# Second attention of a two-block layer: weight pieces over 42 groups, two feature tiles among them, dilated turns in groups 42 to 53

## Chip, cores and metric

The kernel runs on one core of a Trainium2 chip (trn2). The metric is the device time of one execution in microseconds (us); lower is better. Engines: PE (TensorE), DVE (VectorE), ACT (ScalarE), POOL (GpSimd), SP (SyncE, which here only issues the transfers).

## What is computed

One token sequence (512 x 1024, float32) goes through a recurrent layer, a sliding-window attention with sinks, and then a second block, which matters here:

```python
h = rms_norm(x, norm_mix)
proj = h @ w_in
a_q, a_kv, a_g, b_qkv, c_qkv = jnp.split(proj, PROJ_SPLITS, axis=-1)
o_a = nsa_mixer(a_q, a_kv, a_g, ...)       # 4 heads: compressed, selected and window keys
o_b = dilated_mixer(b_qkv, ...)            # 3 dilations x 2 heads, one softmax over all
o_c = stick_breaking_mixer(c_qkv)          # 6 heads, sum of log-failures after each key
x = x + jnp.concatenate([o_a, o_b, o_c], axis=-1) @ w_out
h = rms_norm(x, norm_mlp)
x = x + jnp.square(jax.nn.relu(h @ w_up)) @ w_down
```

## The kernel before, in words

All weights come as units of 128 x 1024 float32. SP loads each into a ring of 4 buffers (`raw`), in the order of the U_ constants (lines 40 to 66); an engine splits it into a rounded high part `wh` and the remainder `wl`; PE multiplies with three matmuls for each product (lines 1236 to 1238: high-high, high-low, low-high). From unit U_GB on POOL makes the splits (`split`, lines 1180 to 1190: a mark, the high part, two halves of the low part). A unit's place is free once PE has counted it in `units_done`, so units are used in the order in which they stand.

The second block's projection consists of token-major groups G0, G4, G1, G2, G3 (4 units each, four token tiles) and feature-major tiles F0 to F6 (1 unit each). F1 and F4, F2 and F5, F3 and F6 are queries and keys of the three stick-breaking head pairs. G1 holds the dilated queries and the gates' logits, G2 the dilated keys, G3 the dilated values. G0, G4, F0, F1, F4, F2, F5 and F3 are multiplied ahead of the second attention. For each F tile DVE scales the bank (`scale_f`, line 2220), ACT writes the high half (`stick_high`, line 1769), DVE the low one (`low_f`, line 2227). The compressed keys are turned once by PE (line 1496) and copied by ACT (line 1807), before the attention's loop.

The second attention (`make_attention(2)`, from line 571) runs over 68 *groups*, each one head's 128 queries against the keys before them: 8 groups of the first stick pair; then 36 groups of the other branch (compressed, selected, window) with the 16 other stick groups among them; and 8 dilated groups (60 to 67). PE, ACT and DVE run the same software pipeline; in *step* i
- PE (line 813): scores of group i + 4, transposes of group i's probabilities (`turn`), their product with the values for group i - 1, then what else is planted at that step;
- DVE (line 1106): bias, mask and maximum for group i + 3 (`mask1`), finishing a head whose last group was i - 2, for a stick group i + 2 the scan over log-failures (`mask2`: lines 1020, 1021, 1025), the copy of even-numbered chunks of transposed probabilities from the bank;
- ACT (line 899): exponentials of group i + 3 (for stick: Abs, Exp, Ln), Exp of a stick group i + 2, the copy of odd-numbered chunks.

A *chunk* is a bank's worth of transposes (up to four blocks), numbered through (`with_chunks`, line 269); even ones lie in bank 3, odd ones in bank 4, and PE waits for chunk c - 2 to be copied before it writes chunk c. Scores go to banks 0, 1, 2 in turn, and from group WIDE_FROM (line 160) on also to bank 7. Until then bank 7 takes the *pieces*: F6, and the G1, G2 and G3 tiles, one token tile in two halves of 12 matmuls each (`piece`, line 1501), at the steps of PIECE_STEPS (line 155). ACT and DVE take a tile one step after its second half (TAKEN, line 157). After G2, `scales` gives the reciprocal norms of the dilated heads.

The twelve dilated tiles (six of queries, six of keys) go through *turns* (TURNS2, line 152): POOL scales and doubles a head pair's rows (`double`, line 1131), PE transposes them as a chunk of its own (`turn_chunk`, line 806, transposes on line 810), ACT copies that chunk one step later (line 915), POOL writes high and low half (`split_dil`, lines 1154 and 1157). There are two buffers: POOL's order is double 0, double 1, split 0, double 2, split 1, and so on. The split of turn 0 waits for the last piece of G3, because the tiles lie where PE's inputs xh and xl were. The dilated groups' scores (from step 56) wait for all twelve. POOL's order is: splits of all units up to G3, the turns, then the units of the output projection (line 1228).

At the end of the loop TAILS (line 164) starts the first output tiles; the output projection and the MLP (from 790 us on) are PE at work without a break.

## Time and profile before

| | |
|---|---|
| median of 3 runs | 1176.36 us (1174.43 to 1176.77) |
| the profiled execution | 1172.59 us, its span 1170.8 us |
| PE busy | 1111.2 us, 95% of the span |
| DVE, ACT, POOL busy | 643.3, 425.5, 529.9 us |
| mean granted PE clock | 0.98 |
| DMA | 97.18 MB, mean 83 GB/s |
| chain that ended last | PE 77%, DVE 12%, ACT 5%, issue 4% |

A time is that of one execution; the span is from the first to the last instruction on the profile. Busy time of PE contains overlap of matmuls in the pipeline. A clock of 1.00 is the upper of PE's two levels (2.4 GHz), 0.5 the lower (1.2 GHz); a mean in between is a mixture in time. In rows, the text in square brackets is how long the engine was idle before an instruction and which one released it; "x12" is a count.

### The profile page before, as it was taken

The numbers are of one execution on the slowest core, as the hardware profiler recorded it, in microseconds if no ns is written. First come the engines' busy times: TensorE is split into PE (matmuls) and PEld (weight loads), VectorE is DVE, ScalarE is ACT, GpSimd is POOL, SyncE is SP. The second block draws the span as 40 slices with busy tenths as digits, with TensorE's granted clock in tenths as the row PEclk, the third lists the DMA queues.
The fourth block names the chain that finished last, engine by engine and source line by source line (L and its number), as shares of the span: only waits on it lengthen the run. The fifth ranks groups of instructions, "written<-read, shape, count | busy, mean of one in ns | idle before, by whom it ended". The sixth has DMA issues, their size and how long they took to land.

```text
span 1170.8 us, 16126 instructions
## 1 busy us (share of the span) xinstructions
PE 1111.2 (95%) x5801; PEld 951.2 (81%) x5801; DVE 643.3 (55%) x1131; ACT 425.5 (36%) x852; POOL 529.9 (45%) x525
## 2 busy tenths in 40 slices
PE   6999999999989999999988977789999999999998
PEld 5788888898779888898888977678878888888887
DVE  6869777677567646484566576845631321321321
ACT  5373668363346532115554565523020110110110
POOL 0000000000443327989454165408976776777772
PEclk9999999999999999999999887899999999999999
DMA  6322322413211002323221000202423223223221
GB/s 247 127 89 90 109 90 90 144 54 126 90 54 38 20 18 72 125 92 127 72 73 55 18 2 1 72 1 91 127 90 100 98 90 108 90 93 104 90 90 54
DMA packets 27280, 97.18 MB, mean 83 GB/s; under 512 B 3024, under 2 KB 3408, under 8 KB 27088
## 3 DMA queue, kind: packets, MB, share of 16 engines
q1 hardware_dynamic: 27216, 96.32, 24.5%
q8 instruction: 41, 0.67, 0.2%
q14 instruction: 23, 0.19, 0.1%
HBM read 94.21 MB, written 2.10 MB: 82 GB/s over the span
## 4 chain that ended last, share of the span: by engine, by line
PE 77%; DVE 12%; ACT 5%; issue 4%; POOL 1%; DMA 1%; SPq 0%; DVEq 0%; POOLq 0%; ACTq 0%
PE bank L1236 22%; PE bank L1238 21%; PE bank L1237 21%; PE bank L788 4%; PE bank L751 4%; PE bank L768 3%; DVE arena L1967 1%; DVE wl L1918 1%; DVE arena L1021 1%; ACT wh L1597 1%; PE bank L810 1%; DVE arena L1006 1%; DMA x<-x_in 1%; POOL wl L1189 0%; DVE arena L2318 0%
## 5 line engine op out<-in xcount | busy, mean ns | idle before, releaser
L1185 POOL TENSOR_TENSOR hold<-hold 128x2 f32<-128x2 f32 x117 | 29.3, 251 | 524.8 <-PE bank L1238 524.8
L1236 PE MATMUL bank<-xh,wh 128*128 128x512 f32 x568 | 226.4, 399 | 12.2 <-DVE xl L1887 9.7
L1238 PE MATMUL bank<-xh,wl 128*128 128x512 f32 x568 | 221.9, 391 | 0.0
L1237 PE MATMUL bank<-xl,wh 128*128 128x512 f32 x568 | 221.9, 391 | 0.0
L1236 PE MATMUL bank<-yh,wh 128*128 128x512 f32 x520 | 203.4, 391 | 2.0 <-DVE yl L2323 1.5
L1238 PE MATMUL bank<-yh,wl 128*128 128x512 f32 x520 | 202.4, 389 | 0.0
L1237 PE MATMUL bank<-yl,wh 128*128 128x512 f32 x520 | 202.3, 389 | 0.0
L1189 POOL TENSOR_TENSOR wl<-raw,wh 128x512 fp32r<-128x512 f32 x117 | 175.3, 1498 | 0.0
L1188 POOL TENSOR_TENSOR wl<-raw,wh 128x512 fp32r<-128x512 f32 x117 | 157.1, 1343 | 9.8
L1236 PEld LDWEIGHTS bank<-xh,wh 128*128 128x128 f32 x568 | 107.2, 189 | 35.5 <-issue 11.9
L1186 POOL TENSOR_SCALAR wh<-raw 128x1024 fp32r<-128x1024 f32 x117 | 126.8, 1084 | 0.0
L1238 PEld LDWEIGHTS bank<-xh,wl 128*128 128x128 f32 x568 | 107.0, 188 | 22.8
L1237 PEld LDWEIGHTS bank<-xl,wh 128*128 128x128 f32 x568 | 107.2, 189 | 21.3 <-issue 0.7
L1236 PEld LDWEIGHTS bank<-yh,wh 128*128 128x128 f32 x520 | 97.6, 188 | 23.2 <-DVE yl L2323 1.9
L1238 PEld LDWEIGHTS bank<-yh,wl 128*128 128x128 f32 x520 | 97.6, 188 | 20.6
L1237 PEld LDWEIGHTS bank<-yl,wh 128*128 128x128 f32 x520 | 97.7, 188 | 19.8
L1851 ACT ACTIVATE arena<-arena 128x512 f32<-128x512 f32 x32 | 20.2, 633 | 243.7 <-DVE arena L2318 243.7
L788 PE MATMUL bank<-arena 128*128 128x64 f32 (+2 forms) x620 | 90.7, 278 | 16.0 <-DVE arena L1081 5.4
L788 PEld LDWEIGHTS bank<-arena 128*128 128x128 f32 x620 | 85.8, 204 | 18.6 <-issue 7.4
L2330 DVE TENSOR_TENSOR x<-bank,x 128x512 f32<-128x512 f32 x32 | 22.1, 692 | 140.8 <-PE bank L1238 140.8
L1918 DVE TENSOR_TENSOR wl<-raw,wh 128x1024 fp32r<-128x1024 f32 x56 | 68.0, 1222 | 40.3 <-ACT wh L1597 40.0
L1236 PE MATMUL bank<-wh,xh 128*128 128x512 f32 (+2 forms) x224 | 85.3, 381 | 0.2
(260 smaller groups left out, 1831.8 us busy)
## 6 DMA issues: line engine op xcount, KB each, us to landing
raw<-weight_units SPq DMA_DIRECT2D x173, 512.0 KB, 3.4
x<-x_in SPq DMA_DIRECT2D x4, 512.0 KB, 8.1
out_fm<-x SPq DMA_DIRECT2D x8, 256.0 KB, 2.0
arena<-tables SPq DMA_DIRECT2D x1, 1024.0 KB, 10.5
...
```

The source lines that it names most:

```text
L751: mm = pe.matmul(out, q, kk, start=t == 0, stop=t == len(terms) - 1 and kind != "stick")
L768: mm = pe.transpose(B[3 + c % 2][:, j * P:(j + 1) * P], col0[:, col:col + P], ident[:])
L788: mm = pe.matmul(out, pt[:, c % slots, j * P:(j + 1) * P], value_ap(g, s_, kb), start=first, stop=total == 0)
L1185: pool.tensor_tensor(hold[:], hold[:], hold[:], ALU.add).then_inc(held, 1)
L1186: pool.tensor_scalar(wh[:, j, :], raw[:, j, :], 1.0, 1.0, ALU.mult, ALU.mult).then_inc(high_done, 1)
L1188: pool.tensor_tensor(wl[:, j, 0:512], raw[:, j, 0:512], wh[:, j, 0:512], ALU.subtract)
L1189: pool.tensor_tensor(wl[:, j, 512:1024], raw[:, j, 512:1024], wh[:, j, 512:1024], ALU.subtract)\
L1236: pe.matmul(out, lh, rh, start=start, stop=False)
L1237: pe.matmul(out, lh, rl, start=False, stop=False)
L1238: return pe.matmul(out, ll, rh, start=False, stop=stop)
L1918: dve.tensor_tensor(wl[:, u % RING, :], raw[:, u % RING, :], wh[:, u % RING, :], ALU.subtract)\
L2330: dve.tensor_tensor(x[:, m, :], B[4 + m % 4][:], x[:, m, :], ALU.add).then_inc(down_read, 1)
```

## The change

It reorders; no arithmetic is added or taken away.
- Pieces lie in steps 1 to 41 and not 0 to 29: G1 at 1 to 8, F3 (in two halves) at 10 and 11, F6 (also in halves) at 12 and 13, G2 at eight steps from 15 to 25, G3 at eight steps from 28 to 41.
- F3 is no longer multiplied before the loop, nor F6 behind the scores of step -2. Their scale, high and low halves on DVE and ACT move along, and their units stand behind those of G1.
- The compressed keys' turn moves from before the loop to the end of PE's step 0, ACT's copy of it to step 1; it uses bank 7 (bank 2 before), F5 bank 5 (bank 0 before), F3 bank 7 (bank 1 before).
- The twelve turns lie in the steps 42 to 53, one in each, and not in every second step from 28 to 50. With a turn's chunk between each two groups' chunks, the chunks of groups 42 to 53 have the numbers 45, 47, ... 67.
- Bank 7 joins the scores at group 47 (step 43), not at group 36 (step 32).

```diff
--- before.py
+++ after.py
@@ -57,10 +57,10 @@
 U_W1 = (U_F4 - 2, U_F4 - 1, U_F4 + 1, U_F4 + 2)
 U_F2 = U_F4 + 3
 U_F5 = U_F2 + 1
-U_F3 = U_F5 + 1
+U_G1 = U_F5 + 1
+U_F3 = U_G1 + 4
 U_F6 = U_F3 + 1
-U_G1 = U_F6 + 1
-U_G2 = U_G1 + 4
+U_G2 = U_F6 + 1
 U_G3 = U_G2 + 4
 U_OUT2 = U_G3 + 4
 U_MLP = U_OUT2 + 8
@@ -149,16 +149,16 @@
 ITEMS1 = {-3: ("gate", 4, 8), 14: ("gate", 5, 6), 30: ("gate", 6, 6), 46: ("gate", 7, 6)}
 
 
-TURNS2 = {28 + 2 * k: key for k, key in enumerate([("q", m) for m in range(6)] + [("k", m) for m in (0, 1, 2, 4, 5, 3)])}
-
-
-PIECE_STEPS = {"G1": (0, 1, 2, 3, 4, 5, 6, 7), "G2": (9, 12, 13, 14, 15, 16, 17, 18), "G3": (20, 23, 24, 25, 26, 27, 28, 29)}
+TURNS2 = {42 + k: key for k, key in enumerate([("q", m) for m in range(6)] + [("k", m) for m in (0, 1, 2, 4, 5, 3)])}
+
+
+PIECE_STEPS = {"G1": (1, 2, 3, 4, 5, 6, 7, 8), "F3": (10, 11), "F6": (12, 13), "G2": (15, 17, 18, 19, 21, 22, 24, 25),
+               "G3": (28, 32, 33, 35, 36, 38, 39, 41)}
 PIECES = {step: (name, q // 2, q % 2) for name, steps in PIECE_STEPS.items() for q, step in enumerate(steps)}
-TAKEN = {PIECE_STEPS[name][2 * t + 1] + 1: (name, t) for name in PIECE_STEPS for t in range(TB)}
+TAKEN = {steps[2 * t + 1] + 1: (name, t) for name, steps in PIECE_STEPS.items() for t in range(len(steps) // 2)}
 GATES_AT = PIECE_STEPS["G1"][-1] + 1
 SCALES_AT = PIECE_STEPS["G2"][-1] + 1
-WIDE_FROM = 36
-F6_HIGH, F6_LOW = 5, 6
+WIDE_FROM = 47
 TURN_LAG, OUT_LAG = 5, 6
 
 TAILS = {1: {-1: ((0, 0, 6),), 0: ((1, 0, 6), (0, 6, 7), (1, 6, 7)), 1: ((2, 0, 4),), TURN_LAG - 1: ((2, 4, 7), (3, 0, 4))},
@@ -197,10 +197,11 @@
     seg2 = [("bout", m, "X") for m in range(8)] + [("G0", t, "A") for t in range(4)] + [("ssq", 2, "N")]
     seg2 += [("F", 0, "D"), ("rstd", 2, "B"), ("F", 1, "D")] + [("G4", t, "A") for t in range(4)]
     seg2 += [("hid", 0, "A"), ("hid", 1, "A"), ("F", 4, "D")] + [("nT", j, "D") for j in range(6)]
-    seg2 += [("hT", 0, "A"), ("F", 2, "D"), ("kc", 0, "A"), ("F", 5, "D"), ("F", 3, "D"), ("kcT", 0, "A"), ("F", 6, "D")]
-    pieces = [(name, t) for name in PIECE_STEPS for t in range(TB)]
-    seg2 += [(name, t, "A") for name, t in pieces]
-    at2 = {key: 7 for key in [("F", 6)] + pieces}
+    seg2 += [("hT", 0, "A"), ("F", 2, "D"), ("kc", 0, "A"), ("F", 5, "D"), ("kcT", 0, "A")]
+    seg2 += [("G1", t, "A") for t in range(TB)] + [("F", 3, "D"), ("F", 6, "D")]
+    seg2 += [(name, t, "A") for name in ("G2", "G3") for t in range(TB)]
+    at2 = {item[:2]: 7 for item in seg2[-15:]}
+    at2["F", 5] = 5
     bank, free, before = {}, {}, {}
     count = {"A": 0, "D": 0}
     for seg, items in ((seg1, ITEMS1), (seg2, {})):
@@ -813,8 +814,6 @@
                 for i in range(-LOOK - 1, ng + OUT_LAG):
                     if 0 <= i + LOOK + 1 < ng:
                         scores(i + LOOK + 1)
-                    if i == -2 and a == 2:
-                        behind_scores()
                     if 0 <= i < ng:
                         turn(i)
                     if 0 <= i - V_LAG < ng:
@@ -830,6 +829,8 @@
                         if q == 0 and before7[key]:
                             pe.wait_ge(*before7[key])
                         item(key, range(KD * q // parts, KD * (q + 1) // parts))
+                    if a == 2 and i == 0:
+                        behind_scores()
                     if a == 2 and i in PIECES:
                         item(*PIECES[i])
                     for m, k0, k1 in TAILS[a].get(i - ng, ()):
@@ -899,12 +900,14 @@
                 for i in range(-LOOK, ng + OUT_LAG):
                     if 0 <= i + LOOK < ng:
                         soft1(i + LOOK)
-                    if a == 2 and i in TAKEN:
+                    if a == 2 and i == 1:
+                        behind_scores()
+                    if a == 2 and i in TAKEN and TAKEN[i][0][0] == "G":
                         item(TAKEN[i])
-                    if a == 2 and i == F6_HIGH:
-
-                        act.wait_ge(s["scores"], groups[7]["strip0"] + 1)
-                        item(("F", "high"))
+                    if a == 2 and i - 1 in TAKEN and TAKEN[i - 1][0][0] == "F":
+                        if TAKEN[i - 1][0] == "F6":
+                            act.wait_ge(s["scores"], groups[7]["strip0"] + 1)
+                        item(TAKEN[i - 1])
                     if a == 2 and i == SCALES_AT + 1:
                         item(("scales", 0))
                     if a == 2 and i - 1 in TURNS2:
@@ -916,8 +919,6 @@
                                        scale=scale).then_inc(chunk_taken(chunk_of[name, m])[0], 1)
                     if 0 <= i + LOOK - 1 < ng:
                         soft2(i + LOOK - 1)
-                    if i == -1 and a == 2:
-                        behind_scores()
                     if 0 <= i < ng:
                         copy_out(i)
                     if a == 1 and i in pairs:
@@ -1110,14 +1111,16 @@
                         finish(groups[i - FIN_LAG]["b"])
                     if a == 2 and i - OUT_LAG in pairs:
                         pair_out(pairs.index(i - OUT_LAG))
-                    if a == 2 and i in (-1, F6_LOW):
-                        item(("F", "scale" if i < 0 else "low"))
+                    if a == 2 and i in TAKEN and TAKEN[i][0][0] == "F":
+                        item((TAKEN[i][0], "scale"))
                     if 0 <= i + LOOK - 1 < ng:
                         mask2(i + LOOK - 1)
                     if 0 <= i < ng:
                         copy_out(i)
-                    if a == 2 and i in TAKEN:
+                    if a == 2 and i in TAKEN and TAKEN[i][0][0] == "G":
                         item(TAKEN[i])
+                    if a == 2 and i - 1 in TAKEN and TAKEN[i - 1][0][0] == "F":
+                        item((TAKEN[i - 1][0], "low"))
                     if a == 2 and i in (SCALES_AT, SCALES_AT + 1):
                         item(("scales", i - SCALES_AT))
                     if a == 1 and 0 <= i - FIN_LAG < ng and i - FIN_LAG == end_of[groups[i - FIN_LAG]["b"]]:
@@ -1490,16 +1493,17 @@
             pe.matmul(bk[0:31, 0:HD], hid[:, 0, 0:31], w2[:, 0:HD], start=True, stop=True)
             pe.matmul(bk[:, HD:2 * HD], ar(A_BIAS4, P), w2[:, HD:2 * HD], start=True, stop=True).then_inc(pe_misc, 1)
             f_tile(5)
-            f_tile(3)
-            pe.wait_ge(heads_normed, 5)
-            free(("kcT", 0))
-            pe.transpose(B[BANK[("kcT", 0)]][:, 0:31], kcd[0:31, :], ident[0:31, 0:31]).then_inc(pe_misc, 1)
-
-            def behind_scores():
-                f_tile(6)
+
+            def turn_compressed():
+                pe.wait_ge(heads_normed, 5)
+                free(("kcT", 0))
+                pe.transpose(B[BANK[("kcT", 0)]][:, 0:31], kcd[0:31, :], ident[0:31, 0:31]).then_inc(pe_misc, 1)
 
             def piece(name, t, half):
 
+                if name in ("F3", "F6"):
+                    f_tile(int(name[1]), range(4 * half, 4 * half + 4))
+                    return
                 u0, width = {"G1": (U_G1, 396), "G2": (U_G2, 384), "G3": (U_G3, 384)}[name]
                 if half == 0:
                     free((name, t))
@@ -1517,7 +1521,7 @@
                     mm.then_inc(piece_done, 1)
 
             pe.wait_ge(mask_ready, 1)
-            ATT2[0](pe, piece, lambda m, ks: output_tile(2, m, ks), behind_scores)
+            ATT2[0](pe, piece, lambda m, ks: output_tile(2, m, ks), turn_compressed)
 
 
             for p in range(ATT2[3]):
@@ -1802,15 +1806,16 @@
             root(31, 1)
             act.preload_act_table_set("natural_log_exp_and_others")
             stick_high(5)
-            stick_high(3)
-            wait_done(act, ("kcT", 0))
-            act.activation(kcT[:, 0:31], B[BANK[("kcT", 0)]][:, 0:31], ACT.Copy, scale=gain("nsa", 1)).then_inc(evac_a, 1)
+
+            def take_compressed():
+                wait_done(act, ("kcT", 0))
+                act.activation(kcT[:, 0:31], B[BANK[("kcT", 0)]][:, 0:31], ACT.Copy, scale=gain("nsa", 1)).then_inc(evac_a, 1)
 
             def later(key):
 
                 name, t = key
-                if key == ("F", "high"):
-                    stick_high(6)
+                if name in ("F3", "F6"):
+                    stick_high(int(name[1]))
                 elif name == "scales":
                     roots[0] += 1
                     act.wait_ge(root_ask, roots[0])
@@ -1831,7 +1836,7 @@
                         act.wait_ge(gates_raw, TB)
                         act.activation(gates[:], gates[:], ACT.Exp, scale=-1.0).then_inc(gates_exp, 1)
 
-            ATT2[1](act, later, lambda: None)
+            ATT2[1](act, later, take_compressed)
 
             for m in range(KD):
                 high_and_square(3, m, (x_new, 2 * KD + m + 1))
@@ -2260,14 +2265,13 @@
                               kcr[0:31, :].unsqueeze(1).to_broadcast([31, 2, HD]),
                               v4[0:31, 1, 0:1], None, ALU.mult).then_inc(heads_normed, 1)
 
-            for j in (5, 3):
-                scale_f(j)
-                low_f(j)
+            scale_f(5)
+            low_f(5)
 
             def item(key):
                 name, j = key
-                if name == "F":
-                    (scale_f if j == "scale" else low_f)(6)
+                if name in ("F3", "F6"):
+                    (scale_f if j == "scale" else low_f)(int(name[1]))
                 elif key == ("scales", 0):
                     v = head_view(0, 12)
                     link(dve.tensor_tensor(rx2[:], rx[:], rx[:], ALU.mult))
```

## Rows read from the trace of the kernel before

**Rows 1.** Windows (stretch, length, busy us by engine), front and steps 0 to 62.
```profile
core 0: us, PE busy (x) PEld busy (x) DVE busy (x) ACT busy (x) POOL busy (x), PEclk, DMA share, GB/s
552.50:568.90 16.40, 14.40 (x68) 11.53 (x66) 9.42 (x17) 6.03 (x15) 15.29 (x16) 1.00 0.38 128
568.90:604.00 35.10, 35.07 (x229) 34.75 (x230) 22.88 (x74) 23.94 (x78) 12.02 (x13) 0.95 0.12 40
604.00:635.70 31.70, 28.39 (x176) 27.34 (x175) 18.37 (x46) 14.46 (x41) 11.71 (x13) 0.95 0.16 52
635.70:673.40 37.70, 32.38 (x197) 31.33 (x197) 22.84 (x54) 15.76 (x40) 11.07 (x12) 0.86 0.14 47
673.40:701.20 27.80, 21.91 (x157) 20.38 (x155) 21.30 (x46) 17.03 (x44) 18.98 (x19) 0.88 0.00 1
701.20:731.60 30.40, 22.99 (x143) 21.83 (x141) 20.28 (x47) 15.83 (x40) 18.54 (x20) 0.78 0.00 1
731.60:764.00 32.40, 25.15 (x158) 22.37 (x157) 26.75 (x75) 17.14 (x55) 13.97 (x13) 0.84 0.21 65
```

**Rows 2.** Timeline of PE (start, us, engine, line), steps 21 and 44.
```profile
644.20 0.58 PE L751 MATMUL bank<-yh 128*128 128x256 f32 x1 [4.70 <-DVE arena L1025]
...
709.32 0.41 PE L788 MATMUL bank<-arena 128*128 128x64 f32 x2 [3.64 <-DVE arena L939]
```

**Rows 3.** Timeline of PE, F tile 6, first two G1 pieces, and what follows each.
```profile
560.73 0.45 PE L1236 MATMUL bank<-xh,wh 128*128 128x512 f32 x1
...
566.29 0.39 PE L751 MATMUL bank<-yh 128*128 128x512 f32 x1
...
569.40 0.42 PE L1236 MATMUL bank<-wh,xh 128*128 128x396 f32 x1
...
573.08 0.40 PE L751 MATMUL bank<-yh 128*128 128x256 f32 x1
...
574.00 0.42 PE L1236 MATMUL bank<-wh,xh 128*128 128x396 f32 x1
...
576.26 0.34 PE L751 MATMUL bank<-yh 128*128 128x384 f32 x1
```

**Rows 4.** Timelines of ACT and DVE: F5's halves, masks of groups 1 and 2.
```profile
554.91 1.34 ACT L1769 ACTIVATE yh<-arena,sides 128x512 fp32r<-128x512 f32 x2 [2.74 <-DVE arena L2224]
...
556.28 1.61 DVE L2235 SCALAR_TENSOR_TENSOR yl<-arena,sides,yh 128x512 fp32r<-128x512 f32 x2 [1.41 <-ACT yh L1769]
...
567.10 0.41 DVE L1020 SCALAR_TENSOR_TENSOR arena<-bank,arena 128x256 f32<-128x256 f32 x1
...
570.22 0.56 DVE L1025 TENSOR_TENSOR arena<-bank,arena 128x384 f32<-128x384 f32 x1
```

**Rows 5.** POOL: two turns on its timeline, and groups from 673.6 to 728.8.
```profile
673.69 0.62 POOL L1154 TENSOR_SCALAR xh<-arena 128x512 fp32r<-128x512 f32 x1 [25.59 <-PE bank L1238]
...
676.92 0.62 POOL L1154 TENSOR_SCALAR xh<-arena 128x512 fp32r<-128x512 f32 x1
...
L1144 POOL TENSOR_TENSOR arena<-arena,v 128x512 f32<-128x512 f32 x10 | 11.9, 1187 | 0.8
...
L1154 POOL TENSOR_SCALAR xh<-arena 128x512 fp32r<-128x512 f32 x7 | 4.3, 617 | 33.1 <-PE bank L1238 25.6 <-ACT arena L915 7.4
```

**Rows 6.** Timelines of PE and ACT: step 28's first matmul, copy of its turn.
```profile
666.03 0.39 PE L751 MATMUL bank<-yh 128*128 128x512 f32 x1
...
669.53 0.67 ACT L915 ACTIVATE arena<-bank,hsc 128x512 f32<-128x512 f32 x1
```

**Rows 7.** Timelines of DVE and POOL: a scan undisturbed and one beside POOL.
```profile
571.76 1.22 DVE L1021 TENSOR_TENSOR_SCAN arena<-ones,arena 128x512 f32<-128x512 f32 x1
...
706.09 2.15 DVE L1021 TENSOR_TENSOR_SCAN arena<-ones,arena 128x512 f32<-128x512 f32 x1
...
705.91 1.26 POOL L1157 TENSOR_TENSOR xl<-arena,xl 128x512 fp32r<-128x512 f32 x1
...
707.25 1.84 POOL L1144 TENSOR_TENSOR arena<-arena,v 128x512 f32<-128x512 f32 x1
```

## Prediction, made before the change was run

> **What bounds the kernel now.** I read the profile's page first: TensorE (PE) is busy nearly all the time in every stretch but one, and the thin slices of PE and the low granted clock lie between 560 and 790 us, which is the second attention. The chain of waits there passes between PE and VectorE (DVE) and names no other engine for long. So I cut that stretch at the starts of PE's loop steps (found in PE's timeline by the widths of the scores) and asked for the windows [rows 1]: the front from the end of F tile 5 to step 0, then steps 0 to 9, 10 to 19, 20 to 29, 30 to 41, 42 to 53, and 54 to 62. What is to be seen: in steps 0 to 9 PE is busy for 35.07 of 35.1 us, so PE sets the pace. In steps 20 to 29 it is idle for 5.3 us. In steps 30 to 41 and 42 to 53, which hold no weight pieces, a step takes 2.3 and 2.5 us, PE is idle for 5.9 and 7.4 us and runs at a mean clock of 0.88 and 0.78 of its upper level, while DVE is busy 21.3 and 20.3 us and is what PE waits for. The stage thus has a PE-bound half with pieces and a DVE-bound half without. The long waits are single ones, 4.70 us for a stick-breaking mask and 3.64 us for a copy [rows 2]: DVE does 8 to 11 us of work in two steps (normalising, finishing a head), and a PE without pieces has nothing to do meanwhile.
>
> **What the parts cost on PE.** A half piece of a G tile is 12 matmuls: from 574.00 to 576.26, 2.3 us at the upper clock level, and 569.40 to 573.08, 3.7 us, at the lower one after a wait. F tile 6 is 24 matmuls from 560.73 to 566.29, 5.6 us, so half an F tile is 2.8 us [rows 3]. The work is only moved: no matmul is added or removed. I sum by stretch, each against its row in [rows 1].
>
> *Front.* F3 and F6, 11.2 us of PE, leave it. F5 is done at 552.5. DVE still has its norm and F5's low half to do, until 557.9 (556.28 + 1.61); ScalarE ends F5's high half at 556.25 and softens group 0 (three activations of 0.3 us from there). Then DVE's masks run one behind the other: about 1.6 us for the first, and 3.7 us for the next two (567.10 to 570.78) [rows 4]. That gives 563.2; ScalarE's exponentials for groups 2 and 4, some 1.5 us, the turned compressed keys' evacuation (0.3 us), and handoffs put G1's first piece, which shares bank 7 with those keys, at about 565.3. PE has been mostly idle, so I charge that piece at the lower clock, 3.7 us: step 2 starts at 569. Before, step 2 starts at 576.26 [rows 3] with the same work done but one piece more (G1 from step 0), and from there to step 10 both versions have seven half pieces. So step 10 starts **7.0 us** earlier. The cover of what PE gives up here is gone: PE waits for DVE's masks, which is already counted. SyncE and GpSimd (POOL) come to the G1 units two units earlier and are ahead of PE; F3 and F6 fall behind G1 in their queues, and POOL's 4 us per unit is done before step 10.
>
> *Steps 10 to 19.* PE is busy 28.4 us, with seven half pieces, 17.5 us with one at the low clock; 10.9 us is the rest [rows 1, 3]. After: four F halves (11.2) and four G2 halves (9.2), 31.3 us with the rest. DVE's load (18.4 us, and about 4 us for the scale and low halves of F3 and F6) stays under it. With 0.2 us of waits, 31.5 against 31.7: **-0.2 us**.
>
> *Steps 20 to 29.* PE is busy 32.4 us with eight half pieces (19.8 us, one at the low clock) and one turn: the rest is 12.0 us, of which I put 1 to the low clock. After, five half pieces: 22.5 us. DVE's 22.8 us are now as many, and come in bursts: finishing a head at 20, and scales, a head and a mask at 26 and 27, where no piece lies. The DVE-bound stretches of before took 1.3 and 1.5 times their DVE busy time [rows 1]; by the lower of these it is 29.5 us against 37.7: **-8.2 us**.
>
> *Steps 30 to 41.* PE is busy 21.9 us; the six turns (3.6 us) leave, and seven half pieces (16.3 us) come: 34.6, of which 1.6 us was low clock that a busy PE does not see. PE-bound, 33.0 us against 27.8: **+5.2 us**. A fourth score bank arrives at group 47 and not 36: the scores then wait for a strip that is three and not four behind, as in steps 0 to 31 of before, whose PE-bound stretch shows 0.03 us idle. I cost it at nothing; the pieces hide it, and without them it is the wait of 4.70 us [rows 2].
>
> *Steps 42 to 53: the turns.* Twelve turns of dilated tiles now stand in twelve steps running, and before in every second step of 23. Each asks PE four transposes, ScalarE one copy of 0.67 us, and POOL one high half, one low half and one doubling. Unhindered, POOL takes 3.23 us from one turn to the next (673.69 to 676.92); its doublings average 1.19 and not 1.05 us, so I take 3.3 [rows 5]. PE's turn k waits for doubling k, which stands behind the split of turn k-2. Before, 4.7 to 5 us between turns covered that; now a step of 2.3 to 2.5 us does not, and **POOL becomes the bound**. From the start of a step with the first turn to the end of ScalarE's copy 4.2 us pass (666.03 to 670.20) [rows 6]; ten more rounds of POOL are 33 us, and the last transposes 0.3: 37.5 us against 30.4, **+7.1 us**. Behind PE's waiting turn stand the next step's scores, and DVE and ScalarE wait for those. In this stretch every group's own chunk gets an odd number (a turn's chunk lies between each two), so ScalarE makes all copies and DVE none: it is relieved, not needed.
>
> *From 54 on.* The last split ends some 4 us after step 54 begins, ahead of the dilated scores of step 56. DVE comes without a backlog (before, PE waits for it here); that is worth the time from step 54's start to its copy, **-1.2 us**. The output units' splits move behind the turns, but were finished 30 us early.
>
> Sum: -7.0 - 0.2 - 8.2 + 5.2 + 7.1 - 1.2 = **-4.3 us**. The profiled execution took 1172.59 us (span 1170.8 and 1.8 around it); the median of the runs is 1176.36, so I carry the difference to the median: **1172 us**.
>
> **Where rows and the Trainium skill differ in price.** At 705.91 POOL subtracts for 1.26 us; DVE's scan, started at 706.09, takes 2.15 us where the same width took 1.22 before, and POOL's next doubling takes 1.84 and not 1.05 [rows 7]. So the two wait for each other. The Trainium skill, GPSIMD Engine Reference, section Specifications, says that SBUF interfaces are shared with VectorE, with contention for instructions with two SBUF inputs. By that rule every such DVE instruction is taken from POOL. By the trace the doublings' average carries 0.1 us per turn. That the whole is paid is the second rival.
>
> **Rivals.** (1) *Slower: the turn's handoffs, not POOL's work, set the round.* Place: steps 42 to 53. With all groups' chunks odd, PE's transposes for group i wait for ScalarE's copy of group i-1, and the copy of a turn's chunk stands in the same queue behind exponentials that wait for DVE. If one such copy (0.67 us [rows 6]) and its handoff fall into each round, it is 4.1 us, ten rounds cost 8 more: 1180. It decides from 3.7 us per round. For it: 7.4 us of gaps before POOL's splits put down to ScalarE [rows 5]. Against: those were at every second step, with nothing asked sooner. 18 in 100. (2) *POOL pays for all of DVE's two-input work*: the scans of four stick groups in these steps (3.3 us, by width from 1.22 [rows 7]) and two heads (1.2 us) on rounds of 3.23: 3 us more, 1175. 15 in 100. (3) *The bursts stay*: steps 20 to 29 keep their 5.3 us idle [rows 1] in a stretch of 33.7 us: 1176, no change. 12 in 100. (4) *POOL keeps up*, because ScalarE and PE are slower than I think anyway or POOL's doubling runs ahead: 30.4 us stay for steps 42 to 53 and 7.1 us come back: 1165. Against it stand the three rows of [rows 5]. 10 in 100.
>
> **How the numbers follow.** My case has 45 in 100, with a range of its own from 1169 to 1175 (2 us on the DVE-bound stretch, 1.5 on the front). The range 1165 to 1180 takes in all rivals' values and leaves out their far halves. A measurement can tell 0.2%, 2.4 us. Faster by that: 0.38 of my case, all of (4), a little of (2) and (3): 0.52. Within it: 0.25. Slower: (1), and what is left of (2), (3): 0.23.
>
> **What would show it.** G1's first piece at about 565 and not 569; step 10 near 597; PE's windows in steps 30 to 41 full and at the upper clock; between the twelve turns 3.2 to 3.4 us each, POOL without idle time from about 697 to 735, and PE waiting in front of the transposes of line 810's function with a low clock. Wrong is the forecast if POOL has gaps of over 0.3 us per turn there (rival 1), if steps 42 to 53 take 31 us (4), or if PE still waits over 3 us two or three times between steps 20 and 41 (3).

## The result, and the profile after

The change makes the kernel slower: 1182.43 us median against 1175.99 us for the kernel before, timed beside it on the same chip; the ratio is 1.0062, 95% interval [1.0044, 1.0081] (ratios are formed from the single executions and can differ by 0.001 from the quotient of the medians). Nine executions of after lie between 1179.24 and 1184.90 us; a tenth took 1593.76 us at a mean clock of 0.65 and is left out of the ratio. The prediction was 1172 us, faster; the time lies 2.4 us above its range. The profiled execution of after took 1184.90 us, so it is one of the longer ones; single executions differ by some 5 us, and with them the mean granted clock (0.978 at 1179.2 to 1179.5 us, 0.972 to 0.974 at 1184.3 to 1184.9).

The page of after, its busy times, PE's slices and granted clock, and the chain that ended last:

```profile
span 1182.8 us, 16127 instructions
PE 1117.8 (95%) x5801; PEld 956.1 (81%) x5801; DVE 636.0 (54%) x1125; ACT 428.6 (36%) x858; POOL 527.4 (45%) x525
PE   6999999999989999998989787799999999999998
PEclk9999999999999999999999897879999999999999
PE 75%; DVE 12%; ACT 5%; issue 5%; POOL 3%; DMA 1%; SPq 0%; DVEq 0%; POOLq 0%; ACTq 0%
```

PE has 5801 instructions in both profiles (the program 16126 before, 16127 after); its busy time rose by 6.6 us with no matmul more. The mean granted clock of the two executions is 0.980 and 0.974, so I put the rise down to matmuls at the lower clock level. POOL's share of the chain rose from 1% to 3%. In after, the code stands a few lines lower: scores L752, values L789, matmuls with weights L1239 to L1241, stick masks L1021 to L1026, the doubling L1147, the splits of the turns L1157 and L1160.

The windows of after, cut at PE's steps as in [rows 1], with the columns given there. The rows are: end of F5 to step 2; steps 2 to 9; 10 to 19; 20 to 29; 30 to 41; 42 to 53; 54 to 62; and three pieces of what follows.

```profile
552.50:567.91 15.41, 9.66 (x45) 8.50 (x44) 12.57 (x23) 10.46 (x26) 8.96 (x9) 0.67 0.31 102
567.91:595.75 27.84, 27.52 (x192) 27.23 (x192) 13.01 (x49) 16.84 (x58) 5.42 (x7) 1.00 0.03 7
595.75:633.74 37.99, 33.67 (x188) 30.01 (x187) 26.31 (x69) 15.26 (x46) 17.90 (x18) 0.96 0.23 80
633.74:663.80 30.06, 24.84 (x156) 24.12 (x155) 19.41 (x44) 13.82 (x37) 17.56 (x18) 0.89 0.22 71
663.80:699.10 35.30, 32.75 (x218) 31.57 (x218) 19.73 (x53) 17.05 (x43) 0.00 (x0) 0.95 0.00 1
699.10:737.10 38.00, 26.24 (x169) 24.42 (x168) 19.57 (x45) 23.06 (x55) 31.40 (x31) 0.82 0.00 1
737.10:766.90 29.80, 23.54 (x145) 20.75 (x144) 21.60 (x63) 15.58 (x49) 19.37 (x20) 0.83 0.22 72
766.90:779.00 12.10, 9.30 (x73) 8.25 (x72) 8.38 (x21) 4.38 (x14) 0.00 (x0) 0.96 0.00 1
779.00:792.00 13.00, 13.00 (x59) 12.24 (x59) 2.06 (x5) 1.58 (x3) 0.00 (x0) 0.51 0.01 1
792.00:800.00 8.00, 8.00 (x47) 6.94 (x46) 0.42 (x1) 0.00 (x0) 0.00 (x0) 1.00 0.00 0
```

Beside the predicted terms (us, after minus before; before's step starts are 576.26, 604.0, 635.7, 673.4, 701.2, 731.6 and 761.9):

| stretch | before | after | difference | predicted |
|---|---|---|---|---|
| start of step 2 | 576.26 | 567.91 | -8.3 | -7.0 |
| steps 2 to 9 | 27.7 | 27.8 | +0.1 | 0 |
| steps 10 to 19 | 31.7 | 38.0 | **+6.3** | -0.2 |
| steps 20 to 29 | 37.7 | 30.1 | -7.6 | -8.2 |
| steps 30 to 41 | 27.8 | 35.3 | **+7.5** | +5.2 |
| steps 42 to 53 | 30.4 | 38.0 | +7.6 | +7.1 |
| steps 54 to 62 | 30.3 | 29.8 | -0.5 | -1.2 |
| step 63 to the end | 408.9 | 415.9 | **+7.0** | 0 |
| sum of the spans | 1170.8 | 1182.8 | +12.0 | -4.3 |

The last line but one is in part this execution's own: for 13 us from 779 on, with PE busy throughout, the granted clock is 0.51 (the lower level), where before's was at the upper. At the start of step 63 after is 5.0 us behind before (766.9 against 761.9). Other kernels with the same work behind step 63 take 410.4 us for it, so about 5.5 of the 7.0 us are this execution's.

PE's waits in steps 1 to 20 and later, from its timeline (start, us, engine, line; in brackets the idle time and its releaser):

```profile
559.30 0.80 PE L752 MATMUL bank<-yh 128*128 128x512 f32 x1 [5.05 <-DVE arena L1026]
...
564.96 0.68 PE L1239 MATMUL bank<-wh,xh 128*128 128x396 f32 x1
...
614.77 0.50 PE L752 MATMUL bank<-yh 128*128 128x512 f32 x1 [1.89 <-DVE arena L1026]
...
617.88 0.47 PE L789 MATMUL bank<-arena 128*128 128x64 f32 x1 [1.85 <-DVE arena L1050]
...
656.18 0.80 PE L752 MATMUL bank<-yh 128*128 128x512 f32 x1 [5.22 <-DVE arena L1026]
...
706.76 0.66 PE L769 MATMUL bank<-ident,arena 128*128 128x128 f32 x2 [3.53 <-ACT arena L898]
...
723.78 1.11 PE L811 MATMUL bank<-ident,arena 128*128 128x128 f32 x4 [2.06 <-POOL arena L1147]
```

G1's first piece starts at 564.96 as forecast (565). Behind step 14 stand two waits that I had not forecast. The wait of 5.22 us at 656 (step 28) is the successor of the 4.70 us one in step 21 [rows 2]: it did not go, it moved. VectorE's burst of the dilated heads' norms, a head's finish and a mask stands behind G2's last piece, now in steps 26 and 27, which hold no piece. e2_spread, with G2 where after has it, waits 5.25 us in step 28; f3_late below, with G2 where before has it, 6.82 us in step 21. Of the twelve turns' transposes (L811), the timeline puts six behind a wait for a doubling, 0.87 to 2.06 us each.

What VectorE does ahead of the two waits of steps 10 to 19, on its own timeline, and then GpSimd beside it:

```profile
611.98 0.69 DVE L2229 SCALAR_TENSOR_TENSOR arena<-bank,rstd 128x512 f32<-128x512 f32 x1 [1.44 <-issue]
612.59 0.55 DVE L1021 SCALAR_TENSOR_TENSOR arena<-bank,arena 128x384 f32<-128x384 f32 x1
613.17 0.96 DVE L1022 TENSOR_TENSOR_SCAN arena<-ones,arena 128x384 f32<-128x384 f32 x1
614.16 0.56 DVE L1026 TENSOR_TENSOR arena<-bank,arena 128x384 f32<-128x384 f32 x1
...
615.36 1.10 DVE L1039 TENSOR_SCALAR rsc<-rsc 128x8 f32<-128x8 f32 x1
...
616.94 0.29 DVE L1050 TENSOR_TENSOR arena<-bank,rsc 128x128 f32<-128x128 f32 x1
```

```profile
615.15 1.28 POOL L1192 TENSOR_TENSOR wl<-raw,wh 128x512 fp32r<-128x512 f32 x1
```

It stands idle for 1.44 us until F6's last half is multiplied (to 611.9), scales it (L2229), and only then does the mask for PE's next scores (to 614.7) and the finish of a compressed head (L1039 to L1050, to 617.8). Within the finish an instruction on 8 columns takes 1.10 us (L1039); it ends at 616.46, just as GpSimd's subtraction beside it ends (616.43). More on that below. PE has no piece in step 14, waits for both, and then runs its next half piece in 3.45 us, partly at the lower clock.

### The profile page after: what moved, and what is told of

Same layout as the page of the kernel before. It is cut to its first block, busy times and chain, and to the rows that moved or that the text cites. A ratio compares the mean times of both kernels' runs of the same rounds, so it can differ in the third digit from the quotient of the medians.

```text
span 1182.8 us, 16127 instructions
## 1 busy us (share of the span) xinstructions
PE 1117.8 (95%) x5801; PEld 956.1 (81%) x5801; DVE 636.0 (54%) x1125; ACT 428.6 (36%) x858; POOL 527.4 (45%) x525
## 4 chain that ended last, share of the span: by engine, by line
PE 75%; DVE 12%; ACT 5%; issue 5%; POOL 3%; DMA 1%; SPq 0%; DVEq 0%; POOLq 0%; ACTq 0%
PE bank L1239 21%; PE bank L1241 21%; PE bank L1240 21%; PE bank L789 4%; PE bank L752 3%; PE bank L769 3%; DVE arena L1022 1%; DVE arena L1972 1%; DVE wl L1923 1%; POOL arena L1147 1%; ACT wh L1601 1%; POOL xh L1160 1%; DVE arena L1007 1%; DMA x<-x_in 1%; POOL wl L1192 0%
## 5 line engine op out<-in xcount | busy, mean ns | idle before, releaser
L1188 POOL TENSOR_TENSOR hold<-hold 128x2 f32<-128x2 f32 x117 | 29.1, 248 | 543.0 <-PE bank L1241 543.0
L1239 PE MATMUL bank<-xh,wh 128*128 128x512 f32 x568 | 226.7, 399 | 12.1 <-DVE xl L1892 9.6
L1241 PE MATMUL bank<-xh,wl 128*128 128x512 f32 x568 | 222.0, 391 | 0.0
L1239 PE MATMUL bank<-yh,wh 128*128 128x512 f32 x520 | 204.0, 392 | 2.9 <-DVE yl L2327 2.4
L1241 PE MATMUL bank<-yh,wl 128*128 128x512 f32 x520 | 202.7, 390 | 0.0
L1239 PEld LDWEIGHTS bank<-xh,wh 128*128 128x128 f32 x568 | 107.2, 189 | 35.1 <-issue 11.9
L1241 PEld LDWEIGHTS bank<-xh,wl 128*128 128x128 f32 x568 | 107.0, 188 | 22.8
L1239 PEld LDWEIGHTS bank<-yh,wh 128*128 128x128 f32 x520 | 97.9, 188 | 24.5 <-DVE yl L2327 3.3
L1241 PEld LDWEIGHTS bank<-yh,wl 128*128 128x128 f32 x520 | 97.8, 188 | 20.6
L1856 ACT ACTIVATE arena<-arena 128x512 f32<-128x512 f32 x32 | 20.3, 633 | 244.8 <-DVE arena L2322 244.8
L789 PE MATMUL bank<-arena 128*128 128x64 f32 (+2 forms) x620 | 93.0, 283 | 3.1 <-DVE arena L1050 1.9
L789 PEld LDWEIGHTS bank<-arena 128*128 128x128 f32 x620 | 88.6, 210 | 4.9 <-DVE arena L1050 2.1
L1239 PE MATMUL bank<-wh,xh 128*128 128x512 f32 (+2 forms) x224 | 85.4, 381 | 0.4 <-ACT arena L1834 0.3
```

Source lines behind the costliest of these rows:

```text
L789: mm = pe.matmul(out, pt[:, c % slots, j * P:(j + 1) * P], value_ap(g, s_, kb), start=first, stop=total == 0)
L1188: pool.tensor_tensor(hold[:], hold[:], hold[:], ALU.add).then_inc(held, 1)
L1239: pe.matmul(out, lh, rh, start=start, stop=False)
L1241: return pe.matmul(out, ll, rh, start=False, stop=stop)
```

## The experiments

Twelve kernels in three groups (e, f and g), each timed beside runs of before of its own (1172.97, 1172.96 and 1173.02 us). The ratios are to these; after's is to the 1175.99 us beside it, so kernels of different groups are compared by ratio. Stretches are in the order of the table: steps 2 to 9, 10 to 19, 20 to 29, 30 to 41, 42 to 53, 54 to 62.

| kernel | median us | ratio, 95% interval | stretches, us |
|---|---|---|---|
| before (its profile) | | | 27.7, 31.7, 37.7, 27.8, 30.4, 30.3 |
| after | 1182.43 | 1.0062 [1.0044, 1.0081] | 27.8, 38.0, 30.1, 35.3, 38.0, 29.8 |
| e1_turns | 1172.62 | 0.9992 [0.9977, 1.0006] | 27.7, 31.7, 37.2, 20.3, 38.8, 28.6 |
| e2_spread | 1180.27 | 1.0058 [1.0033, 1.0083] | 25.5, 30.9, 29.0, 36.6, 38.2, 29.6 |
| e3_halflow | 1177.40 | 1.0041 [1.0024, 1.0057] | 27.9, 38.0, 30.1, 35.3, 33.1, 27.8 |
| e4_mixed | 1176.83 | 1.0032 [1.0016, 1.0048] | 27.8, 40.2, 33.9, 32.8, 28.7, 29.3 |
| f1_front | 1175.75 | 1.0034 [1.0016, 1.0053] | 30.8, 36.2, 39.4, 27.7, 27.5, 31.1 |
| f2_gaps | 1170.12 | 0.9973 [0.9960, 0.9986] | 28.1, 36.1, 36.4, 29.3, 27.3, 29.7 |
| f3_late | 1182.95 | 1.0087 [1.0064, 1.0109] | 27.7, 31.7, 29.1, 36.6, 37.9, 30.3 |
| f4_narrow | 1181.82 | 1.0072 [1.0052, 1.0092] | 27.8, 37.9, 28.9, 36.6, 37.9, 30.4 |
| g1_step14 | 1178.90 | 1.0054 [1.0033, 1.0074] | 27.9, 35.8, 29.7, 35.3, 38.1, 28.7 |
| g2_order | 1179.65 | 1.0045 [1.0029, 1.0062] | 27.9, 37.5, 30.3, 35.3, 38.1, 29.5 |
| g3_stretch | 1167.90 | 0.9940 [0.9917, 0.9963] | 27.8, 36.1, 31.3, 30.2, 29.4, 29.9 |
| g4_beforehalf | 1170.85 | 0.9977 [0.9957, 0.9998] | 28.5, 31.7, 38.7, 25.8, 27.9, 30.7 |

A stretch is from one profiled execution. With the same work it repeats within 0.1 us in steps 10 to 19 (38.0, 38.0 and 31.7 four times), within 1.5 us in steps 20 to 41, and within about 3 us in steps 42 to 62 (before took 30.4 us in 42 to 53 at a clock of 0.78, f1_front with the same work there 27.5 at 0.88). The start of step 2 lies between 575.2 and 577.8 in the five kernels with before's front, and between 567.4 and 572.4 in the nine with after's.

### The turns alone

```diff
 # e1_turns, from before
-TURNS2 = {28 + 2 * k: key ...
+TURNS2 = {42 + k: key ...
```

> The kernel before with the twelve turns alone moved to steps 42 to 53, one each. Theory A (GpSimd's 3.3 us per turn bounds these steps): they take 37 to 38 us and not 30.4, steps 30 to 41 get 1 to 3 us shorter without their six turns, and the kernel is 4 to 6 us slower than before (1180 to 1182). Theory B (the turns are nearly free, the pieces' places cost the time): 0 to 2 us slower, steps 42 to 53 at 31 to 33 us.

The total doesn't change. Steps 42 to 53 grow by 8.4 us, as Theory A has it, and steps 30 to 41 shrink by 7.5 us, where it had 1 to 3:

```profile
674.40:694.70 20.30, 17.14 (x132) 15.31 (x132) 16.01 (x47) 13.13 (x36) 0.00 (x0) 1.00 0.00 1
694.70:733.50 38.80, 27.01 (x172) 25.01 (x170) 20.25 (x47) 24.09 (x58) 31.32 (x31) 0.78 0.00 1
```

So Theory A fell as a price of the change: a turn costs about 1.25 us in steps 30 to 41 (7.5 over 6 turns), not the 0.6 us of PE that I had counted for it, and it is given back in full where the turn leaves. Of the 7.5 us, 4.8 are busy time of PE (21.9 to 17.1, with the clock at 1.00 where it was 0.88) and 2.7 idle time. Without turns these twelve steps take 1.7 us each, and PE is idle for 3.2 us in all: little room for seven pieces of 2.3 us.

### Where the pieces stand

```diff
 # e2_spread, from before (F3, F6 and the compressed keys' turn stay where they are)
 # turns at 42 + k, WIDE_FROM = 47
-"G2": (9, 12, 13, 14, 15, 16, 17, 18), "G3": (20, 23, 24, 25, 26, 27, 28, 29)
+"G2": (15, 17, 18, 19, 21, 22, 24, 25), "G3": (28, 32, 33, 35, 36, 38, 39, 41)
 # f3_late, from before: the same, but G2 as in before
```

> The change without the move of F3, F6 and the compressed keys: G1 stays at steps 0 to 7, G2 and G3 lie as after, turns in 42 to 53, bank 7 for scores from group 47. Theory A: the front's gain of 8 us is lost, but so is the loss of 6 us in steps 10 to 19 that the F tiles' VectorE work makes there, so the kernel is within 2 us of the changed one, some 5 us over before. Theory B (moving the F tiles is what costs): it is 4 us or more faster than the changed kernel.

> Edit, from the kernel before: only G3 moves, to 28, 32, 33, 35, 36, 38, 39 and 41; turns at 42 to 53, bank 7 from group 47. Theory D (a half piece costs PE its full 2.3 us in steps 30 to 41, which without turns have 3 us idle in 20.3; a piece that leaves 20 to 29 gives back less, as VectorE bounds): 30 to 41 take 36 us, 20 to 29 take 26 to 28 us, total 1178 to 1181. Rival G (G2's spreading costs as much as G3's): 1174 to 1176.

e2_spread has nearly the whole loss of after (1.0058 against 1.0062); F3 and F6 need not move for it. Its stretches price their move: steps 10 to 19 take 30.9 us with four half pieces of G2 and no F half, and 38.0 in after with the four F halves added, 7.1 us. The front gains as much by their leaving (7.3 us, the mean start of step 2 in the kernels of each kind: 576.6 and 569.4). And the three half pieces of G2 that e2_spread takes out of steps 10 to 19 give back 0.8 us (31.7 to 30.9), with PE idle for 5.7 us there. f3_late has the loss with G3 alone, by four runs. Their windows: e2_spread's steps 30 to 41, then f3_late's steps 20 to 29 and 30 to 41:

```profile
661.80:698.40 36.60, 34.25 (x217) 32.96 (x217) 19.79 (x53) 17.05 (x43) 0.00 (x0) 0.91 0.02 9
```

```profile
637.00:666.10 29.10, 18.84 (x109) 17.58 (x108) 20.70 (x50) 12.35 (x33) 11.04 (x12) 0.77 0.18 60
666.10:702.60 36.50, 34.18 (x217) 32.91 (x217) 19.74 (x53) 17.05 (x43) 0.00 (x0) 0.91 0.00 1
```

Against e1_turns, f3_late moves seven half pieces from steps 20 to 29 into 30 to 41. It pays 16.3 us there, 2.3 us for each, and gets 8.1 us back, 1.2 us for each: what remains in steps 20 to 29 is VectorE's work, busy 20.7 of 29.1 us in bursts, with PE idle for 10.3 us and at a clock of 0.77. The scores' fourth bank arrives eleven groups later in both. No run moves it alone; 20.3 us and seven pieces of 2.3 us are 36.4 us, and 36.6 were measured, which leaves little for it. Rival G in f3_late's expectation (G2's spreading costs as much) fell: it gave 1174 to 1176 us, and e2_spread, with G2 spread as well, is if anything the faster of the two (the intervals overlap).

### POOL in steps 42 to 53

```diff
 # e3_halflow, from after; g4_beforehalf, the same from before
-pool.tensor_tensor(...[rows, :], src[rows, :], ...[rows, :], ALU.subtract)
+pool.tensor_tensor(...[rows, 0:256], src[rows, 0:256], ...[rows, 0:256], ALU.subtract)
```

> The changed kernel, with GpSimd subtracting only the first 256 of 512 columns in each low half of a dilated tile (the others are left as they were), some 0.6 us less GpSimd work per turn. Theory A (GpSimd's work sets the round): steps 42 to 53 get 5 to 7 us shorter, one round 2.7 us. Theory C (handoffs between TensorE, ScalarE and GpSimd set it): under 2 us shorter, GpSimd idle grows by what its work shrinks.

> Edit, from the kernel before: POOL's low halves of the dilated tiles cover 256 of 512 columns (the others keep old values). With the same edit the kernel after lost 4.9 us in steps 42 to 53. Theory A (POOL is the bound only when the turns stand in every step): before, with turns in every second step, doesn't change, steps 30 to 53 take 57 to 59 us, total within 1 us. Rival S (POOL's work slows VectorE through their shared access, wherever it stands): steps 30 to 53 fall by 3 us or more, total 1169 to 1170.

POOL's groups in steps 42 to 53 (busy, mean ns, idle before and its releaser), first of after, then of e3_halflow:

```profile
L1147 POOL TENSOR_TENSOR arena<-arena,v 128x512 f32<-128x512 f32 x10 | 11.5, 1153 | 0.8
L1160 POOL TENSOR_TENSOR xh<-arena,xh 64x512 fp32r<-64x512 f32 (+1 forms) x7 | 9.0, 1287 | 0.6
```

```profile
L1147 POOL TENSOR_TENSOR arena<-arena,v 128x512 f32<-128x512 f32 x10 | 11.3, 1134 | 0.8
L1160 POOL TENSOR_TENSOR xh<-arena,xh 64x256 fp32r<-64x256 f32 (+1 forms) x7 | 5.8, 825 | 0.6
```

The low half takes 0.46 us less, and the stretch falls from 38.0 to 33.1 us, 0.41 us for each of twelve turns: POOL's work sets the round there, as forecast. (The total shows about half of that, 1.0041 against 1.0062, with intervals that overlap.) In before's arrangement (g4_beforehalf) the two stretches of steps 30 to 53 together are 4.5 us shorter than in before's profile, but only 1.5 us shorter than in f1_front, which has the full low halves (27.7 and 27.5 us), and the total is lower by 2.2 us with an interval that reaches from 0.2 to 5 us. Whether POOL's work slows VectorE there (Rival S) or nothing changes (Theory A) this can't settle.

### Pieces among the turns

```diff
 # e4_mixed, from after
-TURNS2 = {42 + k: ...}
+turns at 34, 36, 38, 40, 42, 43, 45, 47, 48, 50, 51, 53;  WIDE_FROM = 39
-"G2": (15, 17, 18, 19, 21, 22, 24, 25), "G3": (28, 32, 33, 35, 36, 38, 39, 41)
+"G2": (15, 16, 17, 18, 19, 20, 21, 22), "G3": (25, 27, 28, 29, 30, 31, 32, 33)
```

> The changed kernel with its pieces closer (G2 at steps 15 to 22, G3 at 25 and 27 to 33), turns from step 34 to 53 with a step between most of them, bank 7 for scores from group 39. Theory A: the front's 8 us stay, the turns no longer bound steps 42 to 53 (31 to 33 us), the loss in steps 10 to 19 shrinks to 3 or 4 us: 1170 to 1174, faster than both kernels. Theory B (late pieces and three score banks cost the time) expects the same; Theory D (a stage bound by VectorE, which gets nothing back from any order): no faster than before, 1176 or more.

Better than after, but not better than before, and outside the 1170 to 1174 us expected: steps 42 to 53 lose their excess (28.7 us), and steps 10 to 19 get longer still (40.2 us with five half pieces of G2 and four of F tiles, where the loss was expected to shrink to 3 or 4 us). The number is that of Theory D; that no order gives anything back, f2_gaps and g3_stretch below refute.

### F3 and F6

```diff
 # f1_front, from after: turns at 28 + 2k, WIDE_FROM = 36
+"F3": (9, 10), "F6": (11, 12), "G2": (13, ..., 20), "G3": (22, ..., 29)
 # f2_gaps, from after: turns at 30 + 2k, WIDE_FROM = 36, unit and bank order G1, F3, G2, F6, G3
+"F3": (10, 11), "G2": (12, ..., 19), "F6": (21, 22), "G3": (23, ..., 30)
 # f4_narrow, from after
-VectorE's scaling and low halves of F3 and F6 over 512 columns
+over 64 columns
```

> Edit, from the kernel after: F3 at steps 9 and 10, F6 at 11 and 12, G2 at 13 to 20, G3 at 22 to 29, the twelve turns back at 28, 30, ... 50, bank 7 from group 36. So this is the kernel before with F3, F6 and the compressed keys' turn moved behind G1, and G2 packed a little closer. Theory D (the front's 8 us are a loan: the F halves cost PE 11 us again in steps 10 to 29, and VectorE's scaling and low halves stand before the masks there): step 2 starts near 568, step 30 near 673, total within 2 us of before, 1171 to 1175. Rival F (the front's gain is real, and only the spreading of G2 and G3 eats it): step 30 near 667, total 1165 to 1167.

> Edit, from the kernel after: F3 at steps 10 and 11, G2 at 12 to 19, F6 at 21 and 22, G3 at 23 to 30, turns at 30, 32, ... 52, bank 7 from group 36. The F halves stand in the steps in which PE had no piece and waited for VectorE. Theory D: the waits at 20 to 22 (4.7 us before) take up most of F6's 5.6 us, so steps 10 to 29 take 3 to 4 us longer than before (69.4) instead of 8, step 30 starts near 669, and the total is 2 to 4 us under before, 1169 to 1171. Rival: VectorE is the bound there, and its extra work (2 us for a tile) only pushes the masks back: total as before.

> Edit, from the kernel after: VectorE's scaling and its low halves of F3 and F6 cover 64 of 512 columns (these tiles' other columns are not computed); TensorE's and ScalarE's work stays. Theory D (VectorE bounds steps 10 to 19, where after takes 38.0 us against my 31.5): VectorE is busy 3.5 us less there, 10 to 19 take 34 to 35 us, and the total falls by 3 to 4 us to 1178. Rival P (PE's own work and its low clock): 10 to 19 take over 37 us, the total is that of after.

f1_front gains 8.4 us at step 2 and has given back all but 1.4 us at step 63; its total is even above that of before (1175.75 us, just outside the 1171 to 1175 expected). Its steps 10 to 19 are PE-bound (busy 35.5 of 36.3 us). The gain in front is a loan, as Theory D says, where the F halves stand among pieces that fill PE anyway. f2_gaps puts F6 where before has PE waiting for VectorE (step 21, [rows 2]); the wait falls from 4.70 to 2.26 us, and the kernel is 2.8 us under before, as expected.

f4_narrow is the miss that teaches most. VectorE's work for F3 and F6 falls from 3.9 to 1.7 us (its busy time in the stretch by 1.9 us, not the 3.5 expected), and steps 10 to 19 don't shorten at all, as its Rival P had it. But it is not PE's own work that bounds there; the same two waits stand behind step 14:

```profile
619.16 0.50 PE L752 MATMUL bank<-yh 128*128 128x512 f32 x1 [1.73 <-DVE arena L1026]
...
622.26 0.43 PE L789 MATMUL bank<-arena 128*128 128x64 f32 x2 [1.85 <-DVE arena L1050]
```

```profile
616.52 0.23 DVE L2230 SCALAR_TENSOR_TENSOR arena<-bank,rstd 128x64 f32<-128x64 f32 x1 [1.90 <-issue]
```

The scaling takes 0.23 us instead of 0.69, and VectorE stands idle in front of it for 1.90 us instead of 1.44: it waits for F6's last matmul. So 2 us less of work on VectorE are worth nothing here: where it stands in the queue counts more than how much it is.

### Order and cover in step 14

```diff
 # g1_step14, from after
-"G2": (15, 17, 18, 19, 21, 22, 24, 25)
+"G2": (14, 17, 18, 19, 21, 22, 24, 25)
 # g2_order, from after: in VectorE's step, item((F, "scale")) moves
 # from ahead of mask2 and copy_out to behind them
```

> Edit, from the kernel after: the first half piece of G2 at step 14 instead of 15. Theory O (order, not load: after F6's last half in step 13 VectorE stands idle for it until 611.98, scales it, and only then does the mask of 2.1 us and the finish of a head, while PE, without a piece in step 14, waits 1.89 and 1.85 us and then runs a piece at the low clock): PE has a piece to do in that gap; steps 10 to 19 take 34 to 35.5 us instead of 38.0, the total falls by 3 to 4 us, to about 1178. Rival P (PE-bound, the waits are only slack): no change.

> Edit, from the kernel after: VectorE scales an F tile behind the second half of the stick mask and the chunk copy of its step, not ahead of them. Theory O: the mask starts 2.1 us earlier (1.44 idle and 0.69 of scaling no longer ahead of it), PE's waits of 1.89 and 1.85 us and the low clock behind them go; steps 10 to 19 take 34 to 35.5 us instead of 38.0, the total is about 1178. Rival P: 10 to 19 stay over 37 us.

PE's waits of over 0.3 us in steps 13 to 15, in g1_step14 and then in g2_order:

```profile
619.14 0.53 PE L789 MATMUL bank<-arena 128*128 128x64 f32 x2 [1.85 <-DVE arena L1050]
```

```profile
616.84 0.43 PE L789 MATMUL bank<-arena 128*128 128x64 f32 x2 [2.88 <-DVE arena L1050]
```

A piece in step 14 hides the wait for the mask at the start of step 15, and the stretch takes 35.8 us instead of 38.0; the wait for the finish of the compressed head, later in step 15, stays at 1.85 us. With the other order the mask starts about 2 us earlier and its wait goes too, but the wait for the finish grows to 2.88 us, and the stretch is only 0.5 us shorter. Neither reaches the 34 to 35.5 us expected. In total both kernels are a little under after's ratio, by less than the intervals tell.

Two traces show what Theory O leaves out. e2_spread has no F half in these steps and no piece in steps 8 to 14, and the same two waits stand in step 15:

```profile
616.30 0.50 PE L752 MATMUL bank<-yh 128*128 128x512 f32 x1 [1.22 <-DVE arena L1026]
...
618.47 0.43 PE L789 MATMUL bank<-arena 128*128 128x64 f32 x2 [0.92 <-DVE arena L1050]
```

So the waits are there without F3 and F6, and longer with them: 1.89 and 1.85 us instead of 1.22 and 0.92. What lengthens the second is, by the traces, GpSimd. In e2_spread GpSimd is idle during the finish, and its instruction L1039 takes 0.17 us; in after GpSimd splits a unit just then (its place in the ring came free with F6's last matmul), and L1039 takes 1.10 us. The 0.93 us between them are the 0.93 us between the two waits. In g2_order two of the finish's instructions are held:

```profile
613.60 1.05 DVE L1039 TENSOR_SCALAR rsc<-rsc 128x8 f32<-128x8 f32 x1
614.68 0.20 DVE L1040 RECIPROCAL rsc<-rsc 128x8 f32<-128x8 f32 x1
614.92 0.95 DVE L1041 TENSOR_TENSOR rsc<-rsc,gates 128x8 f32<-128x8 f32 x1
```

GpSimd's two subtractions end at 614.62 and 615.85, these two at 614.65 and 615.87. That is most of why the wait grew when the order was changed. No run moves GpSimd's split alone, so this is read from the traces and not tested.

### A version that beats both

```diff
 # g3_stretch, from f2_gaps
-"G3": (23, 24, 25, 26, 27, 28, 29, 30);  turns at 30 + 2k;  WIDE_FROM = 36
+"G3": (23, 24, 26, 27, 29, 30, 32, 33);  WIDE_FROM = 39
+turns at 34, 36, 38, 40, 42, 43, 45, 47, 48, 50, 51, 53
```

> Edit, from the kernel f2_gaps (F3 at 10 and 11, G2 at 12 to 19, F6 at 21 and 22): G3 at 23, 24, 26, 27, 29, 30, 32, 33 and the turns at 34, 36, 38, 40, 42, 43, 45, 47, 48, 50, 51, 53, bank 7 from group 39. If a turn costs 1.2 us wherever it stands (as the first runs show) and a half piece 2.3 us: steps 20 to 29 take 4 us less (32), 30 to 41 3 us more (32), 42 to 53 1 to 2 us more (29): total as f2_gaps, 1168 to 1172. A total over 1175 would say that denser turns cost more than the pieces' place; under 1167 that the pieces fill gaps.

1167.90 us, 0.6% under before and 1.2% under after. Against f2_gaps it is not shown to be faster (0.9940 and 0.9973, the intervals overlap). Its windows for steps 10 to 19, 20 to 29, 30 to 41 and 42 to 53:

```profile
597.50:633.60 36.10, 35.28 (x213) 32.33 (x212) 25.19 (x65) 16.06 (x48) 18.02 (x20) 1.00 0.21 71
633.60:664.90 31.30, 28.13 (x180) 26.12 (x179) 24.49 (x52) 14.96 (x39) 17.04 (x17) 1.00 0.26 84
664.90:695.10 30.20, 26.45 (x185) 24.57 (x184) 18.51 (x47) 16.37 (x42) 10.30 (x10) 0.94 0.00 1
695.10:724.50 29.40, 22.20 (x155) 21.18 (x153) 19.71 (x46) 17.38 (x44) 23.46 (x23) 0.83 0.01 1
```

In steps 10 to 29, PE is idle for 4.0 us (67.4 less 63.4) and never at the lower clock; in after for 9.5 us (68.05 less 58.5). In the same time it does four F halves and thirteen half pieces, where after does four F halves and nine. The four pieces that after has left over it pays for in steps 30 to 41.

## Why the prediction was wrong, point by point

**Front, -7.0 (measured -8.3): right.** Over all profiles of either front it is -7.3, so part of the 8.3 is this execution's. (My own terms gave 7.3: 576.26 less 569.) The first piece came when forecast (564.96 against 565.3); the piece ran at the lower clock for only half of its matmuls and took 2.95 us, not 3.7.

**Steps 10 to 19, -0.2 (measured +6.3): the step that failed.** I summed PE's busy time to 31.3 us and put 0.2 us of waits on it, since VectorE's load "stays under it". Measured were 33.7 us of busy time and 4.3 us of waits. The busy time is 2.4 us over: 0.4 in the F halves (3.0, 2.95, 2.85 and 2.83 us and not 2.8 each), 1.15 in a half piece partly at the lower clock (3.45 us), the rest in other work. The waits are 4.1 us over. Before had 3.3 us of them in the same steps (31.7 less 28.4 [rows 1]), and I took it that the F halves would fill them. They stood in other steps than the waits: step 14 stayed empty, and behind it PE waits 1.89 us for a mask and 1.85 us for a head's finish. Comparing loads (26.3 of 38.0 us on VectorE, and I had expected 22.4) could not have shown these: f4_narrow takes load away and nothing happens, g1_step14 adds cover in step 14 and 2.2 us go, e2_spread has both waits with no F half at all.

What the moved work adds to them is order. VectorE takes its instructions in turn: in after it stands idle for 1.44 us in front of the scaling that waits for F6's last matmul, and the mask behind starts at 612.59, 16.8 us into the stretch; in g2_order, with the scaling behind it, it starts 14.9 us into it. A scaling that waits for a tile's last matmul is a meeting of the two engines, and PE, having just delivered, has no piece in hand. I asked what each moved step adds to a queue, not what it holds up there, nor when GpSimd's split of the next unit would fall.

**Steps 20 to 29, -8.2 (measured -7.6): right in size**, by the factor of 1.3 over VectorE's busy time; here 30.1 us on 19.4 is a factor of 1.55 on less work than I had assumed. Two errors that cancel.

**Steps 30 to 41, +5.2 (measured +7.5): mis-sized.** PE's busy time came out as summed, 32.75 us against 33.0; the term that I set to nothing is 2.55 us of idle time beside it. I had the pieces hide what PE waits for in a stretch without them. They did hide most of what e1_turns has there with no piece: its waits in steps 35, 37 and 39 (0.45, 1.29 and 0.88 us, of 3.2 us idle) are gone. But 1.77 us of new waiting for a mask stand in step 31, behind two steps that hold no piece (29 and 30), and f3_late, with the same places for G3, has the same 1.77 us.

**The exchange between stretches.** Up to step 63 I forecast -4.3 us and +5.0 were measured; of the 9.3 us between them, steps 10 to 19 are 6.5 and steps 30 to 41 are 2.3. But why the kernel is slower as a whole stands in no single term: e2_spread loses as much with F3 and F6 where they were. Moving a half piece out of steps 20 to 29 gives 1.2 us and putting it into 30 to 41 costs 2.3 us (f3_late against e1_turns). The turns, which I blamed for 7.1 us, are free when they move alone (e1_turns, 1172.62 us), since steps 30 to 41 give back 7.5 us; the pieces then take the room that the turns left. Pieces moved on top of the turns cost 8 to 10 us in total (e2_spread, f3_late against e1_turns), and the front's gain of 7 to 8 us is spent again in steps 10 to 19.

**Steps 42 to 53, +7.1 (measured +7.6): right in mechanism, the size in part by luck.** POOL is busy 31.4 of 38.0 us, PE waits for its doublings, and e3_halflow takes 4.9 us off by POOL's work alone. A round took 3.1 to 3.2 us and not 3.3; beside the rounds PE waits 3.53 us for ScalarE (at 706.76), with POOL idle for 2.08 us. And before's 30.4 us are long for their work: against f1_front's 27.5 the turns cost over 10 us. Rival 1 (handoffs set the round) gave 1180, the nearest number of all, by luck: its rounds of 4.1 us are not there. Rival 2 (POOL pays for all of VectorE's two-input work) gave 3 us more than were found: the doublings average 1.15 us here against 1.19 in before [rows 5]. The Trainium skill, GPSIMD Engine Reference, section Specifications, has the two engines share their SBUF interfaces; single rows agree (a doubling of 1.85 us at 704.06 against 1.05 at 710.03). That page gives no price; that GpSimd pays for all of it was my reading, and in steps 10 to 19 the traces show VectorE paying. Rival 4 (POOL keeps up) fell. Rival 3 (the bursts stay) was right in that these steps keep 5.2 us of idle time (30.06 less 24.84), all of it in one wait, now in step 28; it was wrong in the length of the stretch.

**From 54 on, -1.2 (measured -0.5), and the end, 0 (measured +7.0 in the profiled execution).** The latter I could not have priced from one profile; 13 us of it run at 0.51 of the upper clock. e3_halflow, g1_step14, g2_order and f4_narrow, with the same order of work behind step 54, take 410.4 to 410.5 us there, e2_spread 414.5, f1_front 418.7. Even without it after loses 5 us.

The range reached to 1180 because of rival 1; a case "waits among the pieces" on the slower side, which the moved scaling should have suggested, was missing.
